# Attention stages: transposes and row scales of a one-group step issued ahead of the scores of the step two later

## The reference, cut to what matters

```python
# causal attention with a forget gate (16 heads of 64, 1024 tokens), one query block of 128 rows
s = jnp.einsum('bhqd,bhkd->bhqk', qi, kt)
s = s + fqi[..., None] - fk[:, :, None, :]
s = jnp.where(kpos[None, :] <= qpos[:, None], s, -jnp.inf)
p = jax.nn.softmax(s, axis=-1)
return jnp.einsum('bhqk,bhkd->bhqd', p, vt)

# window attention (8 heads, 1024 + 256 tokens): a query block sees its own key block, its two
# neighbours and 256 context keys; the context's own query blocks see the 256 context keys
s = jnp.einsum('bqhgd,bkhd->bhgqk', q, k).astype(jnp.float32) * scale
s = jnp.where(mask, s, NEG_INF)
s = jnp.concatenate([s, sink], axis=-1)
p = jax.nn.softmax(s, axis=-1)
return jnp.einsum('bhgqk,bkhd->bqhgd', p[..., :-1], v)
```

## Time and profile before

| what | value |
|---|---|
| time, median of 3 runs | 4553.06 us (4550.03 to 4554.48) |
| the profiled execution's own time | 4552.95 us |
| its span in the trace | 4551.2 us |
| TensorE matmul busy | 4237.5 us, 93% of the span |
| VectorE, ScalarE, GpSimd busy | 2038.7, 1096.8, 229.7 us |
| granted TensorE clock, mean | 0.966 |

### The profile page before, as it was taken

How to read it: one execution, slowest core, us unless ns; L and a number is a source line. 1 busy time by engine, 2 the same in 40 slices (tenths; PEclk the granted TensorE clock), 3 DMA queues, 4 the chain that set the end, 5 groups by cost and what they waited for, 6 DMA issues and landing times. The chain is left out here.

```text
span 4551.2 us, 62109 instructions
## 1 busy us (share of the span) xinstructions
PE 4237.5 (93%) x24680; PEld 2959.1 (65%) x24680; DVE 2038.7 (45%) x4676; ACT 1096.8 (24%) x2473; POOL 229.7 (5%) x281
## 2 busy tenths in 40 slices
PE   7996899999999999996999999989999995999997
PEld 3443756888667787674888888868757773433342
DVE  5408344433676454746111111124435546666664
ACT  2011222212565323722100000022135532110001
POOL 0100000000221000000000000000000000000000
PEclk8997999999999999997999999999999997999998
DMA  7658210222321112115677777750160014888886
GB/s 276 248 87 338 79 74 34 93 93 102 140 104 55 63 61 94 32 61 227 215 262 266 255 253 256 260 207 22 60 223 20 20 45 173 314 327 322 343 327 221
DMA packets 133310, 756.97 MB, mean 166 GB/s; under 512 B 14080, under 2 KB 52736, under 8 KB 97648
## 3 DMA queue, kind: packets, MB, share of 16 engines
q1 hardware_dynamic: 107600, 669.78, 40.0%
q0 software_dynamic: 20272, 64.76, 5.3%
q10 hardware_dynamic: 5232, 19.63, 1.2%
HBM read 663.46 MB, written 91.19 MB: 166 GB/s over the span
## 5 line engine op out<-in xcount | busy, mean ns | idle before, releaser
L437 PE MATMUL psum<-w_ring,arena 128*128 128x256 f32 (+1 forms) x2784 | 610.1, 378 | 19.3 <-PEq L196 8.3
L437 PEld LDWEIGHTS psum<-w_ring,arena 128*128 128x128 f32 x2784 | 522.4, 191 | 90.6 <-issue 20.8
L3232 PE MATMUL psum<-arena,w_ring 128*128 128x160 f32 x4096 | 563.9, 300 | 3.1 <-ACT arena L3314 3.1
L3232 PEld LDWEIGHTS psum<-arena,w_ring 128*128 128x128 f32 x4096 | 559.7, 191 | 6.3 <-issue 6.3
L437 PE MATMUL psum<-arena,w_ring 128*128 128x256 f32 x1600 | 354.8, 381 | 6.5 <-DVE arena L492 3.5
L437 PEld LDWEIGHTS psum<-arena,w_ring 128*128 128x128 f32 x1600 | 302.8, 191 | 50.6 <-DVE w_ring L533 3.6
L1826 PE MATMUL psum<-arena 64*128 64x256 f32 (+5 forms) x1056 | 288.5, 512 | 9.0 <-PEq L1442 3.5
L3373 DVE TENSOR_TENSOR arena<-arena,psum 128x320 f32<-128x320 f32 x64 | 31.2, 488 | 526.5 <-PE psum L3232 526.5
L409 PE MATMUL psum<-arena,w_ring 128*128 128x512 f32 (+1 forms) x624 | 262.3, 573 | 1.6 <-DVE arena L342 1.6
L1886 ACT ACTIVATE arena<-psum 128x512 f32<-128x512 f32 (+3 forms) x436 | 194.3, 482 | 253.2 <-PE psum L1839 250.4
L1894 ACT ACTIVATE arena<-arena,small 128x640 f32<-128x640 f32 (+8 forms) x272 | 244.6, 900 | 5.8 <-DVE small L1941 5.7
(11 more groups left out here) (435 smaller groups left out, 5257.6 us busy)
## 6 DMA issues: line engine op xcount, KB each, us to landing
w_ring<-in_wstream SPq DMA_DIRECT2D x210, 2048.0 KB, 8.3
arena<-in_wstream SPq DMA_DIRECT2D x49, 2048.0 KB, 7.8
x_rows<-arena SPq DMA_DIRECT2D x26, 512.0 KB, 2.7
w_ring<-in_wstream ACTq DMA_DIRECT2D x6, 2048.0 KB, 8.1
arena<-x_rows SPq DMA_DIRECT2D x18, 512.0 KB, 6.5
xn_rows<-arena POOLq DMA_DIRECT2D x18, 512.0 KB, 7.1
arena<-f_rows SPq DMA_DIRECT2D x8, 1024.0 KB, 7.7
arena<-x_rows SPq DMA_DIRECT2D x8, 1024.0 KB, 9.2
```

What stands on the lines that cost most here:

```text
L437: last = self.cr.nc.tensor.matmul(out, l, r, start=(start and k == 0), stop=(k == len(pairs) - 1), skip_group_check=True)
L3232: last = nc.tensor.matmul(half(bank0 + v)[:, c], w[:, k, m * P:(m + 1) * P], xT[:, k, :], start=(k == 0), stop=(k == KT - 1))
```

## The change

For steps with one group in the two stages, TensorE now issues turn and spread of step s - 2 ahead of the scores of step s, and the values behind them. For steps with two groups the order is what it was. VectorE's place of the first group comes ahead of the maxima of that round in all steps, where it did so only for steps of two groups. Nothing is added or removed.

```diff
-    turn_first = lambda s: not full_keys and len(steps[s].groups) == 2
...
-                if ng and turn_first(s - 2):
-                    turn(goff[s - 2])
-                    for m in range(np_):
-                        scores(s, m)
-                    turn(goff[s - 2] + 1)
-                else:
+                if full_keys:
                     for m in range(max(np_, ng)):
                         if m < np_:
                             scores(s, m)
-                        if m < ng and full_keys:
+                        if m < ng:
                             turn(goff[s - 2] + m)
-                    if ng and not full_keys:
+                    if ng:
+                        spread(s - 2)
+                else:
+                    if ng:
                         turn(goff[s - 2])
-                if ng:
-                    spread(s - 2)
-                    for g in range(ng):
-                        values(goff[s - 2] + g)
+                    if ng == 1:
+                        spread(s - 2)
+                    for m in range(np_):
+                        scores(s, m)
+                    if ng == 2:
+                        turn(goff[s - 2] + 1)
+                        spread(s - 2)
+                for g in range(ng):
+                    values(goff[s - 2] + g)
...
-                early = old and turn_first(s - 2)
+                early = old and not full_keys
```

## The result

The changed kernel takes 4573.4 us (median of 10 runs, 4563.4 to 4583.6), the kernel before 4552.9 us in the same comparison (10 runs, 4550.0 to 4555.6). The ratio is 1.0045 with a 95% interval of 1.0037 to 1.0053: 20.5 us, or 0.45%, slower. The profiled execution took 4577.0 us.

The account below looks back on a forecast made before the run. In the causal stage's short blocks, TensorE's wait for VectorE's inverse was taken to set the pace. 4552.95 us plus 19.0 for eight causal pairs plus 1 for the window stage gave 4573, likeliest range 4566 to 4580, 8 in 10 4561 to 4585.

Parts of the forecast that it names:

- the clock: Causal stage: idle pieces in short blocks bring TensorE to 1.2 GHz for stretches; 8 to 12 us more, up to 4585; chance 0.12.
- The closed chain: Causal one-group blocks: scores, maxima, inverse, spread, next scores set the pace; spreads 1 to 3 wait 2.1, 1.2, 1.5 us.
- The size of a pair: Causal stage: each pair of heads becomes 2.37 us longer, 19.0 us in eight pairs.
- the spread distance of 0.30 us: Time from a spread to the scores behind it, taken as 0.30 us between bounds of 0.27 and 0.42.
- the link from scores(3) to spread(2): Causal pair: 1.27 to VectorE's first read, 1.71 maxima, 0.42 reciprocal and copy, 0.06 to the spread.
- the walk: Causal pair timed from the end of values(7): scores(6) start at 16.82 us, where before it was 14.45.
- The first turn of block 4: Causal pair, last TensorE item ahead of scores(6): taken as 1.1 us.
- The copies: Values' waits for ScalarE's and VectorE's placing copies, 20.1 and 11.6 us in the whole kernel, which the new order can hide.
- the rival "faster": The inverse is in time and only the copies' waits go: all 31.7 us give 4521, half 4537; chance 0.07.
- The window stage: Its round of one-group blocks takes 15.2 us, 0.4 more than before, three times; 1 us in all, bounds -3 and +4.
- rivals 1 and 2: 1: wait for the inverse replaces wait for copies, 4566 to 4580, 0.67. 2: clock falls too, up to 4585, 0.12.
- No collision of the copy with GpSimd: Causal stage: two inverse copies a pair take 0.23 us instead of 0.78; 8.8 us less, 4564; chance 0.09.

Follow-up runs that it names:

- the filled kernel: Changed kernel with 7, 3 and 5 constant products put on TensorE between turn and spread of causal blocks 1, 2 and 3; 4569.5 us.
- The kernel with the gate moved: Changed kernel with GpSimd's causal-stage gate made to wait for the inverse that follows the scaling; 4561.3 us, ratio 1.0022 to the kernel before.

## Why the prediction was right, point by point

The predicted 4573 us met 4573.4. The agreement to the last digit is luck, since a stage that was priced too high (19.0 us, where eight undisturbed pairs make 17.5) and an effect that was left out of the sum (the clock, 3.3) partly cancel, and the runs of the changed kernel lie 20 us apart.

- **The closed chain.** Shown. Spreads forecast at 4.48, 8.24 and 12.94 stand at 4.38, 8.23 and 12.86. The waits of 2.1, 1.2 and 1.5 us are 1.99, 1.07 and 1.22 in an undisturbed pair. In the whole stage they come to 28.6 us where some 38 were forecast: in the first pair and behind a fall of the clock TensorE's own work takes longer and eats up part of the wait. The mla stage takes 277.1 us from its first to its last spread in both profiled executions. Taking the spread out of the chain takes the loss away; shortening one link by 0.55 us twice shortens the pair by 1.10; adding 3.4 us of work into the waits adds nothing to the pairs behind the first.
- **The size of a pair.** 2.37 us forecast, 2.19 measured (34.58 less 32.39), 2.14 in the filled kernel. The largest part of the error is the spread distance of 0.30 us: it is 0.20 behind a short turn (1198.81 to 1199.01) and 0.26 behind a wait (1202.91 to 1203.17). Both are under the lower bound of 0.27 that the sum gave it, which was a duration and not a distance between starts. The other way went the link from scores(3) to spread(2), 3.59 us (1203.17 to 1206.76) for the 3.46 of the walk. The first turn of block 4 took 1.03, not 1.1.
- **The copies.** As said, the idle time put down to them went from 31.7 to 4.5 us. Part of it is in the pair's sum: the spreads wait 4.3 us in a pair, and the pair is only 2.2 longer. But I read the row wrongly when I took all 31.7 us for time that TensorE loses, and 4521 in the rival "faster" rests on that. What the earlier turns and copies give is read from the kernel with the spread behind the scores: 1.35 us a causal pair and 2.03 a window pair, 18.7 us in the two stages.
- **The window stage.** 0.4 us a pair forecast, 0.35 measured (38.01 against 37.66); 1 us in all.
- **The clock,** a rival with 0.12 and no place in the sum: it came too, but small. Over the seven pairs that follow the first, the excess over the undisturbed pair is 3.3 us in the profiled execution (pairs of 35.7, 35.6, 35.1 and 35.2 beside 34.6), against 8 to 12 in the rival. It fell in four of the seven and not in each, and a fall cost 0.5 to 1.1 us and not 1 to 1.5, because part of the slower work went into a wait. Filling the waits gave back 5.8 us between the medians of one comparison (4575.3 to 4569.5). The rival also says that the clock is granted in full in the causal stage of before. It is so behind the first pair; near the stage's start that kernel too has 6.8 us at half clock, which is why has 0.99. The statement that I would be wrong if the clock fell was too strong: rivals 1 and 2 are not exclusive.
- **No collision of the copy with GpSimd, no effect, faster.** None happened by itself. The first of these, made on purpose, gave 1.10 us a pair, the 8.8 us in eight pairs at which it was priced; the run times differ by 12 to 14, and 3.3 of the rest may be the clock, which doesn't fall behind the first pair in the profiled execution of that kernel.
- **What adds up.** In the profiled executions the causal stage grew from 262.9 to 283.9 us, by 21.0: eight pairs at 2.2 us and 3.3 for the clock come to 20.9. The window stage has 1 us more from the first to the last spread. The spans differ by 24.1; the causal stage began 3.8 us later for reasons ahead of it, and the rest came back by 1.7 us behind. What scatters there by some microseconds from run to run was not looked into. The kernel with the gate moved has runs from 4554 to 4568 us. Its profiled execution, with no fall behind the first pair, is the fastest of them; whether its clock fell in the causal stage of the others isn't known, so how much of the scatter is the clock's stays open.

## What to carry to other kernels

When an instruction is moved forward in an in-order queue, list what it waits for and where that stands in the other engine's queue. Here a transpose of 0.2 us was moved ahead of the work that fed the very engine it waited for, and two engines that had run side by side took turns. Move a consumer ahead only as far as its producer doesn't stand behind what the consumer's own successors feed; here the big transposes could go forward, and the small one had to go back. And when the removal of a wait changes nothing, look for the wait that took its place before calling it slack. Last, before a sum of waits ahead of a line is taken for lost time, ask whether it is the matmuls' idle time or the loader's.

## What the runs showed of the hardware that was not expected

Behind the same wait the clock falls in some pairs and not in others. Stretches of the changed kernel in the profiled execution: TensorE's idle time ahead of a spread, and the stretch that began 1.7 us after it.

```profile
1235.30:1237.49 2.19, 0.20 (x2) 0.00 (x0) 2.07 (x9) 1.83 (x6) 0.86 (x2) 1.00 0.03 7
...
1239.20:1246.03 6.83, 6.60 (x35) 4.10 (x32) 4.50 (x20) 2.16 (x6) 0.00 (x0) 0.50 1.00 362
```

TensorE had stood idle for some 2 us, then worked again for 1.7, and then its clock fell to 1.2 GHz although it had work. In the pair before, with the same wait of 1.99 us, the clock stayed at 2.4 GHz (row 1198.53 above). In all it fell in four of the seven pairs behind the first, each time within 1.7 us after the wait of 2.0 us. The other profiled execution of the same kernel shows it at the same distance of 76 us from the first spread:

```profile
1234.14:1240.97 6.83, 6.64 (x35) 4.13 (x32) 4.53 (x20) 2.16 (x6) 0.00 (x0) 0.51 1.04 377
```

The Trainium skill, page "TensorE: Matmul & The Clock Gate", section "What's actually happening", says that the gate looks at activity in a rhythm of its own that doesn't start with the kernel; by that rule equal waits may differ in effect, and in that these rows agree. The repeat is another matter. All four falls stand at the same distances from the first spread in both executions (76, 110, 182 and 216 us), although the stage begins 5 us earlier in the second; a rhythm that knows nothing of the program would give that only by chance. In the kernel with the new order in the causal stage alone they stand at 40, 111 and 145 us. No run here settles what fixes the places.

With products of constants that nobody reads in the waits, the clock stayed at full speed in all pairs behind the first of the profiled execution. But it also did in the kernel with the gate moved, whose waits are 1.44, 1.07 and 0.67 us. How long a wait has to be to bring it down was not measured.
